# A decoder block in fp32r on one core: attention values issued one unit later, 83 unread matmuls fewer, and the early weight blocks split by ScalarE and VectorE

## The chip, the cores and the metric

The kernel runs on one core of a Trainium2 chip, alone. The time is the device time of one execution in microseconds. Before the change it is 3495.51 us, the median of three runs (3493.86 to 3495.92).

## What is computed

Two transformer-like blocks follow each other over 512 tokens of width 1024. The change touches only the first part of the first block, its mixer:

```python
u = rmsnorm(x, attn_norm_pre)
proj = u @ w_in                       # 27 blocks of 128 columns
fq, fk, fv, ff = split(p_fox)         # 8 heads of 64
o_fox = forgetting_attention(fq, fk, fv, ff, fox_forget_bias)
o_rwkv = rwkv7_time_mix(p_rwkv, ...)  # 8 heads of 64
mix = concat([o_fox, o_rwkv]) @ w_out # 8 blocks
h = x + rmsnorm(mix, attn_norm_post)
```

Forgetting attention is softmax attention with a bias from cumulated forget gates, causal. After the mixer come a gated feed-forward part and the whole second block (an HGRN2 and a retention mixer, and a PEER expert layer), whose code is the same before and after.

## The kernel before

**Storage.** Activations lie transposed, features on 128 partitions and 512 tokens along the free dimension, in an arena of 75 tiles. Weights stream from memory as blocks of 128x1024 values (512 KB) into a ring of four slots, `ring`. SyncE issues the load of block n when block n-4 has been used (semaphore `block_used`). Block numbers: 0 to 12 are the attention's input projection (`N_FOX` = 13), 13 to 26 the RWKV part's (`N_RW` = 14), 27 to 34 the output projection (`B_WOUT` = 27), and the feed-forward part starts at 35 (`B_FFN`).

**Splitting.** A product of two fp32 matrices is made from fp32r parts. Each block is rounded to `ring_hi`, and the remainder goes to `ring_lo`. `three` (lines 330 to 335) issues three matmuls per 128x128 piece and 512 tokens: hi by hi, hi by lo, lo by hi. A block is 8 pieces, so 24 matmuls. Who splits a block differs. Block 0 is rounded by ScalarE and its remainder taken by VectorE. Blocks 1 to 34 are split whole by GpSimd (`split`, lines 1410 to 1418, a multiplication by one and a subtraction for each). From block 35 on ScalarE rounds and VectorE subtracts (`dense` on either). `ready(n)` on TensorE (line 319) waits for the remainder.

**The order of the work.** Each engine has its program written out by hand, with semaphores between them.

1. TensorE multiplies block 0, then forms the sums of squares of the input norm (line 362, eight fp32 products with ones), whose squares ScalarE writes into two tiles by turns, then blocks 1 to 14. VectorE takes the norm's reciprocal root (line 1457) and multiplies each finished bank by it (`normed`, line 1495). For RWKV blocks it also shifts by one token and mixes (`shift`, lines 1498 to 1507, the largest operations on lines 1504 and 1506). Among these it works on the forget gates and copies masks (lines 1511 to 1537).
2. TensorE transposes the attention's values (line 403) and makes four rounds of low-rank products for RWKV (lines 409 to 418): two with 64 rows side by side (412, 415), one with 128 (417) and one with 32 (418). ScalarE applies tanh and sigmoid to their inputs and outputs.
3. Attention runs in 32 units u, head u // 4 and query block t = u % 4, with t + 1 key blocks. For each unit the engines do: TensorE the scores (`fox_scores`, lines 448 to 453), VectorE the maximum (1544), ScalarE exp with the row sum (`fox_exp`), VectorE reciprocal and scaling (1550, 1551), TensorE transposes of the probabilities (475), ScalarE the copy of these to SBUF (`fox_copy`), TensorE the product with the values (486). The loop on every engine is one unit ahead with the scores: `fox_scores(u + 1)`, `fox_out(u)`, `rw_prepare(u)`. `fox_out` holds both the transposes and the values, so TensorE waits for the copy in between. The last function prepares RWKV operands: in units 0 to 11 VectorE shifts a block there, in unit 13 TensorE makes 32 tiny head sums (494), and in units 14 to 30 there is a chain of elementwise work and now and then a transpose (502) or a product (519) on TensorE.
4. In units 0 to 11 TensorE also multiplies one RWKV input block, in four quarters around the transposes (`rw_quarter`). From unit 12 on there are none left, and `keep_clock` (lines 337 to 341) issues matmuls of 512 columns whose result is not read: 4 - t before the transposes and 4 - t after them, 100 in all.
5. After the units come the RWKV levels and chunks (lines 526 to 700, 357.6 to 489 us) with `keep_clock` calls of their own, the group norm, and the output projection (`w_out_block`). Its first half of inputs is the attention's, its second half RWKV's, which VectorE and ScalarE split chunk by chunk (`xs_lo`, line 1453) just before.

Helpers that record many operations: ScalarE's activations all have line 965.

Of the kernel before, what the change touches and what calls it, by code (L numbers as in the profile page):

```python
# [118 lines left out]
def build(nc, xt, par_d, cst_d, sel_d, rot_d, rmask_d, small_d, keys_d, wstream, gates_d, hidden_d, out):  # L119
    with ExitStack() as ctx:  # L120
# [91 lines left out]
        split_hi, dense_hi, dense_lo = sem("split_hi"), sem("dense_hi"), sem("dense_split")  # L212
# [103 lines left out]
        def _(pe):  # L316
            st = Steps(pe, pe_s)

            def ready(n, it=0, per=0):

                if n < B_FFN:
                    pe.wait_ge(w_split, it * per + (n + 1))
                elif n < B_U:
                    pe.wait_ge(dense_lo, it * per + (n - B_FFN + 1))
                elif n < B_S:
                    pe.wait_ge(w_split, it * per + (n - B_U + B_FFN + 1))
                else:
                    pe.wait_ge(u_lo, it * per + (n - B_S + 1))
# [127 lines left out]
            def fox_out(u):  # L456
                h, t = units[u]
                m, e = h // 2, h % 2
                bt, bo = bank[6 + u % 2], bank[2 + m % 2]
# [7 lines left out]
                if u >= N_RW - 2:  # L467
                    if u % 8 == 0:
                        pe.wait_ge(fo_out, m)
                    keep_clock(2 + (m + 1) % 2, 4 - t)  # L470
# [9 lines left out]
                if u >= N_RW - 2:  # L480
                    keep_clock(2 + (m + 1) % 2, 4 - t)
# [40 lines left out]
            for u in range(len(units)):  # L522
                if u + 1 < len(units):
                    fox_scores(u + 1)
                fox_out(u)
                rw_prepare(u)

# [433 lines left out]
        def _(act):  # L961
# [50 lines left out]
            for k in range(KD):  # L1012
                act.wait_ge(in_x[k // 2], 16)
                A(XS[k][0], xr(k), ACT.Copy, scale=pp("attn_pre", k)).then_inc(hi_ready, 1)
            for k in range(KD):
                norm_square(0, k, xr)
            norm_root(0)

# [3 lines left out]
            A(z, z, ACT.Ln, bias=1.0).then_inc(fc_ln, 1)  # L1022
            q = N_FOX + N_RW
# [27 lines left out]
            def fox_copy(u):  # L1051
# [6 lines left out]
                if h % 2 == 1 and t == TT - 1:  # L1058
                    act.wait_ge(fo_ready, u + 1)
                    m = h // 2  # L1060
                    A(tile(OF + m), bank[2 + m % 2][:, :], ACT.Copy).then_inc(fo_out, 1)

            def rw_prepare(u):

                if u == 12:
# [17 lines left out]
            for u in range(len(units)):  # L1083
                if u + 1 < len(units):
                    fox_exp(u + 1)
                fox_copy(u)
                rw_prepare(u)

# [41 lines left out]
            for k in range(4):  # L1130
                act.wait_ge(rw_dve, bd + 4 + k + 1)
                A(XS[4 + k][0], tile(ORW + k), ACT.Copy).then_inc(hi_ready, 1)
            for k in range(KD):
                if k == 4:
                    dense(B_FFN)
# [270 lines left out]
        def _(pool):  # L1406

            one = cst[:, CCOL["ones"][0]:CCOL["ones"][0] + 1].to_broadcast([P, D])

            def split(r, n, it, hi_done, lo_done, first=0):  # L1410

                pool.wait_ge(loaded[r], it * 16 + 16)
                pool.tensor_tensor(ring_hi[:, r, :], ring[:, r, :], one, ALU.mult).then_inc(hi_done, 1)
                pool.wait_ge(hi_done, n + 1)
                if first:
                    pool.wait_ge(lo_done, first)
# [3 lines left out]
            pool.wait_ge(in_cst, 16)  # L1420
            def remainder(r, n, lo_done):

                pool.wait_ge(dense_hi, n - B_FFN + 1)
                pool.tensor_tensor(ring_lo[:, r, :], ring[:, r, :], ring_hi[:, r, :].bitcast(F32), ALU.subtract  # L1424
                                   ).then_inc(lo_done, 1)

            pool.sem_inc(split_hi, 1)
            for r in range(1, RING):
                split(r, r, 0, split_hi, w_split, r)
            with pool.Fori(1, B_FFN // RING) as i:  # L1430
                for r in range(RING):
                    split(r, i * RING + r, i, split_hi, w_split)
# [708 lines left out]
```

## Time and profile before

| | |
|---|---|
| median of three runs | 3495.51 us |
| the profiled execution | 3498.85 us, span 3497.0 us |
| mean granted TensorE clock | 0.977 of 2.4 GHz |
| TensorE busy | 3373.8 us (96%) |
| VectorE, ScalarE, GpSimd busy | 1921.3, 1219.7, 286.6 us |
| chain that ended last | TensorE 85%, VectorE 11%, ScalarE 2% |

Times are microseconds from the first instruction unless marked ns. PE is TensorE, DVE VectorE, ACT ScalarE, POOL GpSimd, and L412 is line 412 of the kernel. The span and some 2 us around it make the execution's time. A matmul's printed duration includes its fill and drain, which overlap with the next one, so the distance of two starts tells what one costs. The granted clock is 1.00 when TensorE may run at 2.4 GHz and 0.50 at 1.2 GHz; a mean between says how the stretch is shared out. In brackets behind a row stands how long the engine had been idle before it, and what ended the idle time.

### The profile page before, as it was taken

The numbers are of one execution on the slowest core, as the hardware profiler recorded it, in microseconds if no ns is written. First come the engines' busy times: TensorE is split into PE (matmuls) and PEld (weight loads), VectorE is DVE, ScalarE is ACT, GpSimd is POOL, SyncE is SP. The second block draws the span as 40 slices with busy tenths as digits, with TensorE's granted clock in tenths as the row PEclk, the third lists the DMA queues.
The fourth block names the chain that finished last, engine by engine and source line by source line (L and its number), as shares of the span: only waits on it lengthen the run. The fifth ranks groups of instructions, "written<-read, shape, count | busy, mean of one in ns | idle before, by whom it ended". The sixth has DMA issues, their size and how long they took to land.

```text
span 3497.0 us, 50301 instructions
## 1 busy us (share of the span) xinstructions
PE 3373.8 (96%) x18594; PEld 2733.2 (78%) x18594; DVE 1921.3 (55%) x3675; ACT 1219.7 (35%) x1588; POOL 286.6 (8%) x122
## 2 busy tenths in 40 slices
PE   8999999999989999998999999999999899999998
PEld 6565786887667788887878888888888788888886
DVE  3565444553366633334245899998986344444443
ACT  2222223332355533333233443444444333333332
POOL 6440010000000000000000444100000000000000
PEclk9887999999999999999999999999999999999999
DMA  4110002332222222222323344455556765555542
GB/s 140 44 47 0 3 19 68 97 97 95 85 72 68 70 73 77 72 73 84 97 90 109 112 144 139 140 180 181 181 180 202 237 206 192 193 194 194 192 144 78
DMA packets 146028, 408.31 MB, mean 117 GB/s; under 512 B 11224, under 2 KB 43992, under 8 KB 143584
## 3 DMA queue, kind: packets, MB, share of 16 engines
q1 hardware_dynamic: 73520, 265.85, 25.1%
q10 hardware_dynamic: 72368, 140.68, 11.2%
q8 instruction: 77, 1.26, 0.1%
q14 instruction: 63, 0.52, 0.1%
HBM read 337.28 MB, written 69.21 MB: 116 GB/s over the span
## 4 chain that ended last, share of the span: by engine, by line
PE 85%; DVE 11%; ACT 2%; issue 1%; ACTq 1%; DMA 0%; DVEq 0%; SPq 0%
PE bank L333 23%; PE bank L335 23%; PE bank L334 23%; PE bank L924 2%; PE bank L429 2%; PE bank L922 2%; PE bank L362 1%; PE bank L858 1%; ACT arena L965 1%; DVE arena L1946 1%; PE bank L486 1%; PE bank L341 1%; PE bank L448 1%; DVE arena L1909 1%; DVE arena L1910 1%
## 5 line engine op out<-in xcount | busy, mean ns | idle before, releaser
L333 PE MATMUL bank<-xs,ring_hi 128*128 128x512 f32 x2488 | 998.0, 401 | 39.4 <-DVE xs L1453 13.8
L335 PE MATMUL bank<-xs,ring_lo 128*128 128x512 f32 x2488 | 975.4, 392 | 0.0
L334 PE MATMUL bank<-xs,ring_hi 128*128 128x512 f32 x2488 | 974.3, 392 | 0.0
L965 ACT ACTIVATE arena<-bank 128x512 f32<-128x512 f32 (+4 forms) x584 | 392.1, 705 | 1031.0 <-PE bank L335 736.6
L965 ACT ACTIVATE ring_hi<-ring 128x1024 fp32r<-128x1024 f32 x469 | 495.9, 1060 | 602.1 <-DMA ring<-weights 367.3
L333 PEld LDWEIGHTS bank<-xs,ring_hi 128*128 128x128 f32 x2488 | 471.2, 189 | 149.4 <-issue 24.8
L1707 DVE TENSOR_TENSOR ring_lo<-ring,ring_hi 128x1024 fp32r<-128x1024 f32 x212 | 258.5, 1224 | 538.6 <-ACT ring_hi L965 537.6
L334 PEld LDWEIGHTS bank<-xs,ring_hi 128*128 128x128 f32 x2488 | 471.6, 190 | 100.0 <-issue 5.3
L335 PEld LDWEIGHTS bank<-xs,ring_lo 128*128 128x128 f32 x2488 | 470.2, 189 | 101.5
L1959 DVE TENSOR_TENSOR ring_lo<-ring,ring_hi 128x1024 fp32r<-128x1024 f32 x206 | 252.4, 1225 | 386.1 <-ACT ring_hi L965 386.1
L333 PE MATMUL bank<-gw,ring_hi 128*128 128x512 f32 x1024 | 398.5, 389 | 0.7 <-ACT arena L965 0.7
L334 PE MATMUL bank<-gw,ring_hi 128*128 128x512 f32 x1024 | 398.3, 389 | 0.0
L335 PE MATMUL bank<-gw,ring_lo 128*128 128x512 f32 x1024 | 398.3, 389 | 0.0
L1424 POOL TENSOR_TENSOR ring_lo<-ring,ring_hi 128x1024 fp32r<-128x1024 f32 x50 | 131.7, 2633 | 1542.7 <-ACT ring_hi L965 1542.7
L333 PEld LDWEIGHTS bank<-gw,ring_hi 128*128 128x128 f32 x1024 | 192.3, 188 | 41.0 <-ACT arena L965 1.1
L335 PEld LDWEIGHTS bank<-gw,ring_lo 128*128 128x128 f32 x1024 | 192.3, 188 | 39.9
L334 PEld LDWEIGHTS bank<-gw,ring_hi 128*128 128x128 f32 x1024 | 192.3, 188 | 39.8
L1978 DVE TENSOR_SCALAR oneL<-cst,arena 128x128 fp32r<-128x128 f32 x512 | 175.4, 343 | 0.0
L1977 DVE TENSOR_SCALAR oneH<-cst,arena,ghi 128x128 fp32r<-128x128 f32 x512 | 175.3, 342 | 0.0
L965 ACT ACTIVATE gw<-arena 128x512 fp32r<-128x512 f32 x128 | 80.5, 632 | 228.9 <-DVE arena L1992 227.3
L1998 DVE TENSOR_TENSOR gw<-arena,gw 128x512 fp32r<-128x512 f32 x128 | 88.3, 692 | 90.8 <-ACT gw L965 90.8
L965 ACT ACT_TABLE_LOAD x89 | 114.2, 1283 | 18.3 <-PE bank L335 9.3
(281 smaller groups left out, 3689.2 us busy)
## 6 DMA issues: line engine op xcount, KB each, us to landing
ring<-weights SPq DMA_DIRECT2D x503, 512.0 KB, 3.6
hidden<-arena ACTq DMA_DIRECT2D x128, 256.0 KB, 4.1
gates<-arena ACTq DMA_DIRECT2D x16, 2048.0 KB, 6.6
arena<-hidden ACTq DMA_DIRECT2D x16, 2048.0 KB, 10.4
arena<-gates ACTq DMA_DIRECT2D x16, 2048.0 KB, 17.3
xres<-x_t ACTq DMA_DIRECT2D x4, 512.0 KB, 6.3
out_t<-arena SPq DMA_DIRECT2D x4, 512.0 KB, 2.9
arena<-ret_decay ACTq DMA_DIRECT2D x1, 1024.0 KB, 5.9
```

What stands on the lines that cost most here:

```text
L333: pe.matmul(out_, wh, x[0], start=start, stop=False, skip_group_check=True)
L334: pe.matmul(out_, wh, x[1], start=False, stop=False, skip_group_check=True)
L335: return pe.matmul(out_, wl, x[0], start=False, stop=stop, skip_group_check=True)
L429: mm = pe.matmul(quad(dst, p, j, g), quad(l, p, j, g), quad(r, p, j, g), start=True, stop=True, skip_group_check=True)
L922: pe.matmul(dst, oneH[:, u % NHOT, j, :], oneB[:, u % NHOT, j, :], start=True, stop=False, skip_group_check=True)
L965: return act.activation(out_, in_, f, **kw)
L1424: pool.tensor_tensor(ring_lo[:, r, :], ring[:, r, :], ring_hi[:, r, :].bitcast(F32), ALU.subtract).then_inc(lo_done, 1)
L1707: TTN(ring_lo[:, r, :], ring[:, r, :], ring_hi[:, r, :].bitcast(F32), ALU.subtract).then_inc(dense_lo, 1)
L1959: TTN(ring_lo[:, r, :], ring[:, r, :], ring_hi[:, r, :].bitcast(F32), ALU.subtract).then_inc(u_lo, 1)
L1977: TSM(oneH[:, u % NHOT, j, :], iota, key1, ghi[:, 0, t1].bitcast(F32), ALU.is_equal, ALU.mult)
L1978: ins = TSM(oneL[:, u % NHOT, j, :], iota, key1, arena[:, PTT + 2, t1], ALU.is_equal, ALU.mult)
L1998: TTN(GW[b][j][1], tile(HV + 8 * b + j), GW[b][j][0].bitcast(F32), ALU.subtract).then_inc(ex_lo, 1)
```

## The change

On TensorE, the product with the values leaves `fox_out` and becomes `fox_values`, issued for unit u - 1 behind the scores of unit u + 1 and ahead of the transposes of unit u. Of the unread matmuls one per unit stays, ahead of the transposes, in units 13 to 31 except 16 and 24: 17 instead of 100. ScalarE's copy of a finished pair of heads moves behind the exp of the next unit. GpSimd's splitting of blocks 1 to 34 is deleted. ScalarE rounds them and VectorE takes the remainders, at places written into their programs, and `dense_hi` and `dense_lo` now count from block 1.

```diff
@@ TensorE, ready and fox_out
-                if n < B_FFN:
-                    pe.wait_ge(w_split, it * per + (n + 1))
+                if n == 0:
+                    pe.wait_ge(w_split, 1)
                 elif n < B_U:
-                    pe.wait_ge(dense_lo, it * per + (n - B_FFN + 1))
+                    pe.wait_ge(dense_lo, it * per + n)
...
-                if u >= N_RW - 2:
-                    if u % 8 == 0:
-                        pe.wait_ge(fo_out, m)
-                    keep_clock(2 + (m + 1) % 2, 4 - t)
+                if u > N_RW - 2 and u % 8:
+                    keep_clock(2 + (m + 1) % 2, 1)
                 pe.wait_ge(fnorm, u + 1)
...
-                if u >= N_RW - 2:
-                    keep_clock(2 + (m + 1) % 2, 4 - t)
+
+            def fox_values(u):
+                h, t = units[u]
+                m, e = h // 2, h % 2
+                bo = bank[2 + m % 2]
                 pe.wait_ge(ft_out, u + 1)
...
             for u in range(len(units)):
                 if u + 1 < len(units):
                     fox_scores(u + 1)
+                if u:
+                    fox_values(u - 1)
                 fox_out(u)
                 rw_prepare(u)
+            fox_values(len(units) - 1)
@@ ScalarE
+            dense(1)
+            dense(2)
             for k in range(KD):
                 norm_square(0, k, xr)
             norm_root(0)
+            for n in range(3, N_FOX):
+                dense(n)
...
             A(z, z, ACT.Ln, bias=1.0).then_inc(fc_ln, 1)
+            for n in range(N_FOX, N_FOX + 4):
+                dense(n)
...
             def rw_prepare(u):
 
+                if u < N_RW:
+                    dense(N_FOX + 4 + u)
...
+                if u and u % 8 == 0:
+                    pair_copy(u // 8 - 1)
                 fox_copy(u)
                 rw_prepare(u)
+            pair_copy(NPAIR - 1)
...
+            dense(B_WOUT + 4)
+            dense(B_WOUT + 5)
             for k in range(KD):
+                if k == 2:
+                    dense(B_WOUT + 6)
                 if k == 4:
+                    dense(B_WOUT + 7)
                     dense(B_FFN)
@@ GpSimd
-            pool.sem_inc(split_hi, 1)
-            for r in range(1, RING):
-                split(r, r, 0, split_hi, w_split, r)
-            with pool.Fori(1, B_FFN // RING) as i:
-                for r in range(RING):
-                    split(r, i * RING + r, i, split_hi, w_split)
-            for n in range(B_FFN // RING * RING, B_FFN):
-                split(n % RING, n, n // RING, split_hi, w_split)
@@ VectorE
+            def dense(n, it=0, per=0):
+
+                r = n % RING
+                ve.wait_ge(dense_hi, it * per + n)
+                TTN(ring_lo[:, r, :], ring[:, r, :], ring_hi[:, r, :].bitcast(F32), ALU.subtract).then_inc(dense_lo, 1)
+
...
+            dense(1)
             ve.wait_ge(in_cst, 16)
             norm_root(0)
+            dense(2)
...
             for n in range(8):
                 normed(n, tile(Q0 + n), bank[n % NBANK])
+                dense(n + 3)
             shift(8, 0)
+            dense(11)
...
             for n in range(11, N_FOX):
                 normed(n, tile(VF0 + n - 9), bank[n % NBANK])
+                dense(n + 3)
...
             shift(N_FOX, 1)
+            dense(N_FOX + 3)
             shift(N_FOX + 1, 2)
...
                 if 1 <= u <= N_RW - 2:
                     shift(N_FOX + 1 + u, 2 + u)
+                if u < N_RW:
+                    dense(N_FOX + 4 + u)
...
+            for n in range(B_WOUT + 4, B_FFN):
+                dense(n)
             for b in range(3):
                 dense(B_FFN + b)
```

## Rows read from the trace of the kernel before

**Rows 1.** Windows: PE, PEld, DVE, ACT, POOL busy; granted clock; DMA share; GB/s

```profile
100.50:133.80 33.30, 27.24 (x60) 9.15 (x58) 9.68 (x9) 12.74 (x22) 8.07 (x4) 0.63 0.05 16
133.80:229.00 95.20, 95.20 (x427) 69.91 (x426) 66.96 (x92) 13.29 (x38) 51.46 (x22) 0.98 0.20 61
...
246.00:357.60 111.60, 99.76 (x337) 57.83 (x338) 54.21 (x126) 28.05 (x72) 0.00 (x0) 0.74 0.00 1
357.60:489.00 131.40, 125.02 (x3723) 109.92 (x3722) 56.15 (x99) 31.39 (x59) 0.00 (x0) 1.00 0.01 4
```

**Rows 2.** Groups, TensorE, 246 to 357.6 us: busy, mean ns | idle before

```profile
L341 PE MATMUL bank<-ring_hi 128*128 128x512 f32 x86 | 34.9, 508 | 0.0
...
L475 PE MATMUL bank<-cst,arena 128*128 128x128 f32 x47 | 11.4, 355 | 9.9 <-DVE arena L1551 9.5
```

**Rows 3.** Timeline, low-rank products: start, duration, engine, line [idle before]

```profile
100.55 1.91 PE L403 MATMUL bank<-cst,arena 128*128 128x128 f32 x16
105.97 1.17 PE L412 MATMUL bank<-arena 64*128 64x512 f32 x1 [3.51 <-ACT arena L965]
...
110.59 2.07 PE L417 MATMUL bank<-arena 128*128 128x512 f32 x2 [2.55 <-ACT arena L965]
...
120.61 1.22 PE L412 MATMUL bank<-arena 64*128 64x512 f32 x1
...
126.62 1.22 PE L412 MATMUL bank<-arena 64*128 64x512 f32 x1
...
130.29 1.12 PE L418 MATMUL bank<-arena 32*128 32x512 f32 x2
```

**Rows 4.** Timeline, VectorE: one operation without and beside GpSimd's work

```profile
71.50 0.75 DVE L1506 SCALAR_TENSOR_TENSOR arena<-arena,par 128x512 f32<-128x512 f32 x1
...
101.98 2.65 DVE L1506 SCALAR_TENSOR_TENSOR arena<-arena,par 128x512 f32<-128x512 f32 x1
```

**Rows 5.** Timeline, the start

```profile
15.01 1.89 POOL L1413 TENSOR_TENSOR ring_hi<-ring,cst 128x1024 fp32r<-128x1024 f32 x1 [14.56 <-DMA ring<-weights]
...
17.09 7.42 PE L362 MATMUL bank<-arena,cst 128*128 128x512 f32 x16
...
19.29 1.90 POOL L1413 TENSOR_TENSOR ring_hi<-ring,cst 128x1024 fp32r<-128x1024 f32 x1
...
23.94 0.79 PE L333 MATMUL bank<-xs,ring_hi 128*128 128x512 f32 x1
...
25.43 3.35 DVE L1457 RECIPROCAL arena<-arena 128x512 f32<-128x512 f32 x1 [11.42 <-ACT arena L965]
```

**Rows 6.** Page's groups: a block rounded by ScalarE, remainder by VectorE

```profile
L965 ACT ACTIVATE ring_hi<-ring 128x1024 fp32r<-128x1024 f32 x469 | 495.9, 1060 | 602.1 <-DMA ring<-weights 367.3
...
L1707 DVE TENSOR_TENSOR ring_lo<-ring,ring_hi 128x1024 fp32r<-128x1024 f32 x212 | 258.5, 1224 | 538.6 <-ACT ring_hi L965 537.6
```

**Rows 7.** Timeline, units 12 and 13

```profile
239.27 0.69 PE L475 MATMUL bank<-cst,arena 128*128 128x128 f32 x2 [2.71 <-DVE arena L1551]
...
242.21 3.88 PE L494 MATMUL bank<-cst,arena 128*128 128x2 f32 x32
```

**Rows 8.** Timeline, unit 17, TensorE at 2.4 GHz

```profile
268.08 0.91 PE L341 MATMUL bank<-ring_hi 128*128 128x512 f32 x3
269.54 0.44 PE L475 MATMUL bank<-cst,arena 128*128 128x128 f32 x2 [0.55 <-DVE arena L1551]
269.73 0.94 PE L341 MATMUL bank<-ring_hi 128*128 128x512 f32 x3
...
271.19 1.12 PE L519 MATMUL bank<-arena,cst 128*128 128x512 f32 x2
```

**Rows 9.** Timeline, unit 29, TensorE at 1.2 GHz

```profile
344.44 0.69 PE L475 MATMUL bank<-cst,arena 128*128 128x128 f32 x2
...
347.38 1.58 PE L519 MATMUL bank<-arena,cst 128*128 128x512 f32 x2
```

**Rows 10.** Timeline, end of the mixer: TensorE waiting for VectorE

```profile
515.94 0.79 PE L333 MATMUL bank<-xs,ring_hi 128*128 128x512 f32 x1 [0.95 <-DVE xs L1453]
```

More of the change, by code:

```diff
@@ L211, in build @@
         w_split = sem("weights_split")
-        split_hi, dense_hi, dense_lo = sem("split_hi"), sem("dense_hi"), sem("dense_split")
+        dense_hi, dense_lo = sem("dense_hi"), sem("dense_split")
         first_hi = sem("first_block_hi")
@@ L319, in ready @@
             def ready(n, it=0, per=0):
-                if n < B_FFN:
-                    pe.wait_ge(w_split, it * per + (n + 1))
+                if n == 0:
+                    pe.wait_ge(w_split, 1)
                 elif n < B_U:
-                    pe.wait_ge(dense_lo, it * per + (n - B_FFN + 1))
+                    pe.wait_ge(dense_lo, it * per + n)
                 elif n < B_S:
-                    pe.wait_ge(w_split, it * per + (n - B_U + B_FFN + 1))
+                    pe.wait_ge(w_split, it * per + (n - B_U + 2))
                 else:
@@ L458, in fox_out @@
                 m, e = h // 2, h % 2
-                bt, bo = bank[6 + u % 2], bank[2 + m % 2]
+                bt = bank[6 + u % 2]
                 if u == 0:
@@ L1057, in fox_copy, with pair_copy @@
                 A(tile(PT0 + u % 2)[:, 0:n], bank[6 + u % 2][:, 0:n], ACT.Copy).then_inc(ft_out, 1)
[L1058 to L1061, printed above, removed]
+            def pair_copy(m):
+                act.wait_ge(fo_ready, 8 * (m + 1))
+                A(tile(OF + m), bank[2 + m % 2][:, :], ACT.Copy).then_inc(fo_out, 1)
             def rw_prepare(u):
+                if u < N_RW:
+                    dense(N_FOX + 4 + u)
                 if u == 12:
@@ L1406, in _, with remainder @@
         def _(pool):
[L1408 to L1416, printed above, removed]
+            def remainder(r, n, lo_done):
+                pool.wait_ge(dense_hi, n)
                 pool.tensor_tensor(ring_lo[:, r, :], ring[:, r, :], ring_hi[:, r, :].bitcast(F32), ALU.subtract
                                    ).then_inc(lo_done, 1)
[L1420 to L1425, printed above, removed]
-            pool.sem_inc(split_hi, 1)
-            for r in range(1, RING):
-                split(r, r, 0, split_hi, w_split, r)
-            with pool.Fori(1, B_FFN // RING) as i:
-                for r in range(RING):
-                    split(r, i * RING + r, i, split_hi, w_split)
-            for n in range(B_FFN // RING * RING, B_FFN):
-                split(n % RING, n, n // RING, split_hi, w_split)
             first = -(-B_U // RING)
@@ L1526, in _ @@
                 normed(n, tile(VF0 + n - 9), bank[n % NBANK])
+                dense(n + 3)
             ve.wait_ge(in_small, 32)
@@ L1702, in _ @@
             xs_lo(1, lambda k: tile(ORW + k - 4), KD - 1)
-            def dense(n, it=0, per=0):
-                r = n % RING
-                ve.wait_ge(dense_hi, it * per + (n - B_FFN + 1))
-                TTN(ring_lo[:, r, :], ring[:, r, :], ring_hi[:, r, :].bitcast(F32), ALU.subtract).then_inc(dense_lo, 1)
+            for n in range(B_WOUT + 4, B_FFN):
+                dense(n)
             for b in range(3):
```

## The prediction

> **What bounds the kernel now.** The windows view comes first, for the granted clock and the busy time by stage. All the code that changes runs before 533 us; what follows is only shifted. TensorE is busy for nearly all of every stretch [rows 1], so a gain must come from idle time of TensorE, from work taken off it, or from a better clock. Two stretches stand out. From 100.5 to 133.8 us (low-rank products) the clock averages 0.63 of 2.4 GHz, and from 246 to 357.6 us (attention units 14 to 31) it averages 0.74. In the second, the groups by line show what fills TensorE: 86 unread matmuls (line 341) and a wait of 9.9 us for VectorE's probabilities [rows 2]. In the low-rank stretch the timeline shows TensorE waiting 3.51 us for an activation and 2.55 us for the next one [rows 3]. Those follow VectorE's token shift, whose last operation takes 2.65 us beside GpSimd's splitting and 0.75 us alone [rows 4]. GpSimd is off the path by its own busy time, yet it stretches operations that are on it.
>
> **The change, part by part.** Times are those of the profiled execution: span 3497.0, whole 3498.9, which is 3.3 above the median of the runs, 3495.5.
>
> *A. The start.* Block 1 landed at 15.0 (GpSimd's wait ends there); block 2 had landed by 19.29, when GpSimd took it up without idle time [rows 5]. ScalarE now splits both before it squares the inputs, and it does so in order, so the first square waits for block 2's landing. A copy takes 1.06 us and a remainder 1.22 [rows 6]. The squares start between 16.1 (block 2 already there) and 20.4. I take a landing midway, 17.2, so squares from 18.2 and the first of the eight summing products at 18.9 instead of 17.1. Their pace, 7.4 us for the eight, is set by the exchange of two buffers and stays. Block 1 starts 1.8 later. Behind the root, VectorE runs the reciprocal (3.35 us, beginning 1.5 after block 1 starts [rows 5]) and only then block 2's remainder. That ends 6.1 us after block 1 began, while a block takes 5.45 (14 of them lie between 23.94 [rows 5] and 100.55 [rows 3]), so block 2 waits 0.7 or 0.8. Cost: **+2.6** (bounds 0 and +5). From there to 100.5 TensorE never waits. A block takes 5.45 us, while VectorE needs 0.7 for the evacuation and 1.2, and ScalarE 1.1, for each, so the steady part is worth nothing either way. If that cover were gone, each late microsecond would count once for each of 25 blocks.
>
> *B. The low-rank stretch.* Without GpSimd, VectorE's shift step falls from 5.0 us to about 2.4 (the operation of [rows 4] is the largest part of that), and the casts and small copies ahead of them get shorter too. The remainders added, 1.2 us for each block, take back less than that. The shift of block 13 then ends some 3 us before block 14 does. The 3.51 us wait goes, and of the 2.55 us some 0.5 stay (ScalarE has four copies and a sigmoid to do). More follows. Before, the clock was at 2.4 GHz up to this idle time and at 1.2 GHz after it, and the stretch ran so until 130. A round took 6.0 us (120.61 to 126.62, like two of the other three [rows 3]), and the only product that ran at 2.4 GHz, line 418 in the last round, took 1.05 us (130.29 to 131.34) instead of 2.0. If the idle time is gone I expect the clock to hold, as it held until this idle time: rounds of 3.05. New: 2.0 for the transposes, 1.0, 0.5, 2.05, three more rounds 9.15, and 2.3 for the first two units' scores, together 17.0 against 33.3. Gain: **16.2**. At the other bound the clock falls anyway: 3 × 3.0 + 2.5 less, so 4.7.
>
> *C. Units 0 to 11.* TensorE carries a block per unit and is busy 95.2 of 95.2 us in just under 12 units, 8.0 for each [rows 1]. ScalarE gets a copy and VectorE a remainder, while VectorE's shift loses some 3 us, so it has less to do than before. The one new wait is VectorE's for ScalarE's copy, which is behind the unit's transposes in the middle of the unit. Queued behind it is the next maximum, and behind that the probabilities for which TensorE's transposes wait. By my count the remainder ends 7.4 us into a unit of 8.0, and the next maximum is not wanted for another 2. Hidden: **0** (a gain is excluded because TensorE has no wait to lose). SP issues the same loads at the same block counts.
>
> *D. Units 12 and 13.* Transposes of unit 13 wait 2.71 us for VectorE, whose shift has an operation of 2.7 us beside GpSimd there as in the stage before [rows 4, 7]. The shift shrinks by 2 to 4 us and a remainder adds 1.2. The fillers and values between unit 12's transposes and the next scores (2.4 us) and, in unit 13, the 2.9 us between transposes (239.27) and head sums (242.21) leave the front [rows 7]. I get transposes 3.0 earlier and head sums 5.6 earlier: **5.6** (bounds 3 and 7). The head sums still precede a stretch at 1.2 GHz.
>
> *E. Units 14 to 31.* The values of unit u-1 now run while VectorE makes the probabilities of unit u, and of 86 fillers 16 remain. In unit 17 the scores end where line 341 starts, 268.08; transposes follow at 269.54, a filler again 0.19 later, and the next stage at 271.19 [rows 8]. The gap before the transposes, 1.46 us, is VectorE's (maximum, reciprocal, scaling) and stays. It takes in 0.36 of values and one filler of 0.23. Behind the transposes 1.65 shrink to 0.2: 1.45 gained. At 1.2 GHz, unit 29 has 2.94 there [rows 9] and keeps 0.35: 2.6 gained. The other 16 units have the same pattern with one to four blocks. Two prices go against it. VectorE's preparation (2.2 to 2.7 us) now reaches past the next scores in every second unit at 2.4 GHz, 0.75 each. At 1.2 GHz the values of a four-block unit (1.9) overfill the gap. Averaged over the four kinds, a unit of 5.2 us at 2.4 GHz becomes 4.0, and one of 7.7 at 1.2 GHz becomes 5.4. The old mean, 111.6 / 18 = 6.2, is 60% of the first and 40% of the second, which makes half of the time slow, as the clock of 0.74 says. With the fillers gone the clock will be low more often. I take two thirds of the units: 4.93 × 18 = 88.7, and 4 for unit 31's late values and the roots of unit 14: 92.7. Gain: **19** (bounds 10 with all at 1.2 GHz, 33 with nearly all at 2.4). It is a judgement that the share goes from 40% to 67%, since the old 0.74 had 34.9 us of fillers in it.
>
> Here a rule of the Trainium skill speaks against the change. "TensorE: Matmul & The Clock Gate", section "A second HAM failure mode: psum-queue depth-cycling", says that TensorE's short idle times between groups of matmuls make its clock swing, and that the throughput pays for it. By that rule all 18 units would be slow, and the gain 10 instead of 19, which is the second rival. The trace agrees that the clock swings here, at 0.74 even with the fillers.
>
> *F. The output projection.* VectorE's split of the mixer's output is stretched beside GpSimd like its shifts, and TensorE waits for it twice, a microsecond each, after the second time at 1.2 GHz [rows 10]. Without GpSimd the chunks are ready before they are wanted: two waits and three chunks at half clock, **3.9** (bounds 2 and 4). Blocks 31 to 34 are copied by ScalarE ahead of its evacuations. Each has landed some 4 us after its slot came free and is wanted 5 to 15 us later: 0.
>
> Sum: +2.6 - 16.2 - 5.6 - 19.0 - 3.9 = -42.1, so 3498.9 - 42.1 = 3456.8, or 3454 at the scale of the median.
>
> **The rivals.**
> 1. *The clock falls in the low-rank stretch all the same.* For it: the stretch stayed at 1.2 GHz for 20 us although TensorE was busy, so these products do not bring the clock back and may not hold it. Against it: the fall came after idle time. B gives 4.7: 3466.
> 2. *Units 14 to 31 sit at 1.2 GHz* for want of fillers: E gives 10.4 instead of 19: 3463. For it: 0.74 with fillers [rows 1]. Against it: the same work is packed into less time, which the fillers had been padding.
> 3. *They stay at 2.4 GHz*, the denser schedule making up for the fillers: E gives 33 or so, 3440.
> 4. *VectorE binds in units 0 to 11*, because the remainder waits for ScalarE's copy behind the transposes. One microsecond in each of 12 units: 3466.
> 5. *Slower.* Without fillers the clock does not come back after unit 31, and the RWKV levels and chunks, 357.6 to 489, run at 1.2 GHz. They are 125 us of TensorE work in 131.4 at clock 1.00 [rows 1], so all of it would cost up to 125: 3579. From 42 us, a third of the stretch, the gain is eaten. Against it: that stretch is dense and has fillers of its own.
>
> That the split does not move is excluded by the diff, and GpSimd's part there is deleted.
>
> **How the numbers follow.** Forecast (A to F as summed) 0.52; rival 1 0.15; rival 2 0.15; rival 3 0.08; rival 4 0.06; rival 5 0.04. A measurement of this kernel can tell about 0.2%, 7 us, from no change. All cases but the fifth are faster by more, and of the fourth a part could be worse than priced: faster 0.94, same 0.02, slower 0.04. The range goes from rival 3 with a little more in A, 3438, to rivals 1 and 2 together, 3474.
>
> **What would show it.** Right: no GpSimd work before the expert blocks; line 1506 of before at 0.75 us throughout; 100.5 to 133.8 at a clock near 1.0 and about 17 us long, after a start 2 to 3 us later; a unit of 4 to 5.5 us after 14 with transposes waiting for the scaling; units 0 to 11 still 8.0. Wrong: a low clock after the 16 transposes, TensorE waiting for remainders in units 0 to 11, or a clock under 1.0 past unit 31.

## The result, and the profile after

| | before | after |
|---|---|---|
| median of 5 runs each | 3495.51 us (3479.96 to 3498.06) | 3456.26 us (3453.43 to 3460.98) |
| ratio | | 0.9897, 95% interval 0.9881 to 0.9913 |
| profiled execution, span | 3498.85, 3497.0 | 3453.43, 3451.6 |
| clock, mean | 0.977 | 0.981 |

The changed kernel is 1.0% faster. The forecast was 3454 us. The profiled execution after is the fastest of its five, and that of before lay 3.3 us above the median, so the two profiles are 45.4 us apart and the medians 39.3.

The page's busy times after. GpSimd is down from 122 operations to 54, all of them far behind this stage; TensorE has 83 instructions fewer, the unread matmuls (100 before, 17 now).

```profile
PE 3342.3 (97%) x18511; PEld 2717.8 (79%) x18511; DVE 1904.2 (55%) x3709; ACT 1253.7 (36%) x1622; POOL 131.7 (4%) x54
```

The windows of the changed kernel (columns as in [rows 1]): the low-rank stretch up to the first quarter of a block, units 14 to 31, the RWKV levels and chunks, the output projection.

```profile
102.76:119.89 17.13, 16.83 (x59) 6.76 (x58) 2.64 (x6) 11.44 (x19) 0.00 (x0) 1.00 0.10 31
229.07:316.18 87.11, 81.37 (x272) 46.46 (x271) 53.66 (x126) 27.65 (x72) 0.00 (x0) 0.70 0.00 1
318.50:449.00 130.50, 124.40 (x3715) 109.14 (x3714) 55.86 (x98) 30.86 (x59) 0.00 (x0) 1.00 0.02 4
449.00:494.00 45.00, 45.00 (x206) 35.78 (x205) 20.72 (x30) 16.66 (x24) 0.00 (x0) 0.96 0.18 59
```

Against [rows 1]: the low-rank stretch has halved and its clock went from 0.63 to 1.00. Units 14 to 31 shrank from 111.6 to 87.1 us, with a clock that did not rise (0.74, then 0.70). The RWKV levels and chunks behind them did not change (131.4 and 130.5 us in these windows, both at 1.00); the output projection did, by some 5 us (step F below).

The timeline at the start. The first copy waits for block 1's landing and the second for block 2's, so the summing products (L362) start at 18.82 (17.09 before) and block 1 (L333) at 25.75 (23.94).

```profile
14.83 1.06 ACT L969 ACTIVATE ring_hi<-ring 128x1024 fp32r<-128x1024 f32 x1 [2.45 <-DMA ring<-weights]
17.10 1.06 ACT L969 ACTIVATE ring_hi<-ring 128x1024 fp32r<-128x1024 f32 x1 [1.21 <-DMA ring<-weights]
18.82 7.49 PE L362 MATMUL bank<-arena,cst 128*128 128x512 f32 x16 [0.94 <-ACT arena L969]
25.75 0.80 PE L333 MATMUL bank<-xs,ring_hi 128*128 128x512 f32 x1
```

The low-rank products on TensorE. Of the waits of 3.51 and 2.55 us [rows 3] only 0.30 is left, and rounds follow each other in 3.17 us where they took 6.0.

```profile
102.76 1.91 PE L403 MATMUL bank<-cst,arena 128*128 128x128 f32 x16
104.60 0.69 PE L412 MATMUL bank<-arena 64*128 64x512 f32 x1
...
106.03 1.13 PE L417 MATMUL bank<-arena 128*128 128x512 f32 x2 [0.30 <-ACT arena L969]
...
108.14 0.69 PE L412 MATMUL bank<-arena 64*128 64x512 f32 x1
...
111.30 0.69 PE L412 MATMUL bank<-arena 64*128 64x512 f32 x1
...
117.63 0.49 PE L448 MATMUL bank<-arena 64*128 64x128 f32 x2
```

Units 12 and 13. The wait for VectorE is 1.77 us (2.71 in [rows 7]), but the 32 head sums (L495) now take 6.34 us instead of 3.88: the clock falls half a microsecond into them, and the window from their start to the next scores has a mean of 0.54.

```profile
220.26 0.49 PE L341 MATMUL bank<-ring_hi 128*128 128x512 f32 x1
222.52 0.44 PE L473 MATMUL bank<-cst,arena 128*128 128x128 f32 x2 [1.77 <-DVE arena L1562]
222.79 6.34 PE L495 MATMUL bank<-cst,arena 128*128 128x2 f32 x32
229.07 2.07 PE L448 MATMUL bank<-arena 64*128 64x512 f32 x2
```

```profile
222.79:229.07 6.28, 6.28 (x34) 6.26 (x33) 3.74 (x4) 2.61 (x3) 0.00 (x0) 0.54 0.00 0
```

### The profile page after: what moved, and what is told of

Its sections match the earlier page's. It is cut to its first block, busy times and chain, and to the rows that moved or that the text cites. A ratio compares the mean times of both kernels' runs of the same rounds, so it can differ in the third digit from the quotient of the medians.

```text
span 3451.6 us, 50061 instructions
## 1 busy us (share of the span) xinstructions
PE 3342.3 (97%) x18511; PEld 2717.8 (79%) x18511; DVE 1904.2 (55%) x3709; ACT 1253.7 (36%) x1622; POOL 131.7 (4%) x54
## 4 chain that ended last, share of the span: by engine, by line
PE 85%; DVE 11%; ACT 2%; issue 1%; ACTq 1%; DMA 1%; DVEq 0%; SPq 0%
PE bank L333 24%; PE bank L335 23%; PE bank L334 23%; PE bank L928 2%; PE bank L429 2%; PE bank L926 2%; PE bank L362 1%; PE bank L862 1%; ACT arena L969 1%; DVE arena L1956 1%; DVE arena L1919 1%; DVE arena L1920 1%; DVE arena L1922 1%; PE bank L448 1%; DVE arena L1954 1%
## 5 line engine op out<-in xcount | busy, mean ns | idle before, releaser
L333 PE MATMUL bank<-xs,ring_hi 128*128 128x512 f32 x2488 | 997.4, 401 | 37.8 <-DVE xs L1452 11.8
L969 ACT ACTIVATE ring_hi<-ring 128x1024 fp32r<-128x1024 f32 x503 | 531.7, 1059 | 660.6 <-DMA ring<-weights 423.2
L1486 DVE TENSOR_TENSOR ring_lo<-ring,ring_hi 128x1024 fp32r<-128x1024 f32 x246 | 300.0, 1224 | 563.3 <-ACT ring_hi L969 562.2
L333 PEld LDWEIGHTS bank<-xs,ring_hi 128*128 128x128 f32 x2488 | 470.3, 189 | 149.2 <-issue 26.8
L1969 DVE TENSOR_TENSOR ring_lo<-ring,ring_hi 128x1024 fp32r<-128x1024 f32 x206 | 252.3, 1225 | 386.9 <-ACT ring_hi L969 386.7
L333 PE MATMUL bank<-gw,ring_hi 128*128 128x512 f32 x1024 | 398.5, 389 | 0.7 <-ACT arena L969 0.7
L333 PEld LDWEIGHTS bank<-gw,ring_hi 128*128 128x128 f32 x1024 | 192.2, 188 | 40.9 <-ACT arena L969 1.1
```

The source lines that it names most:

```text
L333: pe.matmul(out_, wh, x[0], start=start, stop=False, skip_group_check=True)
L969: return act.activation(out_, in_, f, **kw)
L1486: TTN(ring_lo[:, r, :], ring[:, r, :], ring_hi[:, r, :].bitcast(F32), ALU.subtract).then_inc(dense_lo, 1)
L1969: TTN(ring_lo[:, r, :], ring[:, r, :], ring_hi[:, r, :].bitcast(F32), ALU.subtract).then_inc(u_lo, 1)
```

## The experiments

Twelve kernels were run, each against the kernel before on the same chip. "Split" says who splits blocks 1 to 34: GpSimd, or ScalarE and VectorE as in the changed kernel (new). "Values" says whether a unit's product with the values stands right behind its own transposes (at once) or one unit later (late). "D" is the time from unit 13's scores to unit 15's, "E" from there to the transposes behind unit 31, both from the profiled execution, with E's granted clock. "Unread" counts the unread matmuls in units 12 to 31. D and E are of one execution each. That execution lay within 5 us of its kernel's median, save for start_order (7.8 above) and attn_only (7.2 below).

| kernel | split | values | unread | D | E, clock | median us | ratio, 95% interval |
|---|---|---|---|---|---|---|---|
| before | GpSimd | at once | 100 | 16.0 | 111.6, 0.74 | 3495.5 | 1 |
| split_only | new | at once | 100 | 12.4 | 105.8, 0.81 | 3467.2 | 0.9916 (0.9900 to 0.9933) |
| filler_only | new | at once | 17 | 17.2 | 125.6, 0.54 | 3494.1 | 0.9991 (0.9981 to 1.0001) |
| attn_only | GpSimd | late | 17 | 15.9 | 86.2, 0.72 | 3473.5 | 0.9939 (0.9922 to 0.9955) |
| changed kernel | new | late | 17 | 13.6 | 87.1, 0.70 | 3456.3 | 0.9897 (0.9881 to 0.9913) |
| no_unread | new | late | 0 | 13.0 | 89.6, 0.63 | 3459.2 | 0.9900 (0.9884 to 0.9915) |
| once_ahead | new | late | 42 | 12.8 | 78.8, 0.85 | 3443.5 | 0.9849 (0.9835 to 0.9862) |
| order_only | new | late | 92 | 12.0 | 80.8, 0.96 | 3444.8 | 0.9854 (0.9837 to 0.9870) |
| start_order | new, new start | late | 92 | 12.0 | 82.1, 0.94 | 3440.8 | 0.9843 (0.9830 to 0.9857) |
| unfed_once | new, new start | late | 49 | 12.0 | 78.8, 0.85 | 3436.1 | 0.9842 (0.9823 to 0.9860) |
| fed_once | new, new start | late | 57 | 16.0 | 75.5, 0.89 | 3438.6 | 0.9837 (0.9823 to 0.9851) |
| fed_full | new, new start | late | 100 | 14.9 | 81.4, 0.95 | 3443.7 | 0.9852 (0.9836 to 0.9868) |
| fed_one | new, new start | late | 38 | 14.6 | 87.2, 0.70 | 3457.5 | 0.9880 (0.9859 to 0.9902) |
| pool_beside | new, GpSimd busy | late | 17 | 14.3 | 90.5, 0.65 | 3468.6 | 0.9926 (0.9907 to 0.9944) |

### The two parts, each alone

**split_only** is the changed kernel with attention's order and unread matmuls as before. The diff is against the changed kernel (the values' matmuls stand in fox_out again, the pair's copy in fox_copy):

```
-                if u > N_RW - 2 and u % 8:
-                    keep_clock(2 + (m + 1) % 2, 1)
+                if u >= N_RW - 2:
+                    if u % 8 == 0:
+                        pe.wait_ge(fo_out, m)
+                    keep_clock(2 + (m + 1) % 2, 4 - t)
...
+                if u >= N_RW - 2:
+                    keep_clock(2 + (m + 1) % 2, 4 - t)
...
-                if u:
-                    fox_values(u - 1)
```

> The early weight blocks split by ScalarE and VectorE as in the changed kernel; attention's order, its unread matmuls and the pair copies as before. Theory: the steps of the changed trace add up, so this one carries the start (+2.2 us), the low-rank stretch (-16), units 0 to 11 (-0.6) and the output projection (-5): about -19.5 us, 3476 us (3472 to 3480), and its low-rank rounds take 3.2 us each at granted clock 1.00. Rival: the low-rank stretch is faster only because everything near it moved with the attention part; then its rounds are still 6 us and the kernel gains only some 4 us, 3491 us.

3467.2 us: 29.6 below before in its series, 10 more than the steps allow. The low-rank rounds are 3.2 us at 1.00, as expected. Most of the surplus stands in units 12 to 31 although their code is before's: D 12.4 for 16.0, and E 105.8 for 111.6 with a clock of 0.81 for 0.74. Another 8.4 us lie behind unit 31 (there, 3467.4 - 336.4 against 3497.0 - 357.6), where the steps had 5: 5.6 in the output projection, as in the changed kernel, 0.9 in the RWKV stage, and 1.9 in all that follows. What follows is the same code in every kernel here and took between 2938.6 and 2942.6 us in their profiles, so the 1.9 says nothing.

**attn_only** is before's code with the attention part of the diff and nothing else.

> Only the attention part: values one unit later, one unread matmul in each late unit; GpSimd still splits the early blocks. Theory of added steps: units 14 to 31 give their -24.5 us and units 12 and 13 some -3: 3468 us (3464 to 3472); the low-rank rounds stay at 6.0 us each. Rival: the two parts help each other (the clock at the entry into unit 14 depends on the split), then the gain here is under 20 us, over 3476 us.

3473.5 us, between the two: the gain is 23.3. E is 86.2, as in the changed kernel. The first low-rank round and most of the second run at the low clock, the last two at 2.4 GHz (L412 at 105.45, 113.89, 119.19, 122.35), so the stretch from the first transpose to the first scores was 25.5 us long and before's 30.8, though its code and its wait of 3.52 us were the same. Most of the 5.3 us between them are the clock's. The parts alone give 29.6 and 23.3, together 39.3: they overlap.

### The attention part taken apart

**order_only** and **filler_only** fill the square: with the new split, the order of the values and the number of unread matmuls are changed one at a time. In order_only (the second hunk stands behind the unit's own transposes):

```
-                if u > N_RW - 2 and u % 8:
-                    keep_clock(2 + (m + 1) % 2, 1)
+                if u >= N_RW - 2 and u % 8:
+                    keep_clock(2 + (m + 1) % 2, 4 - t)
...
+                if u >= N_RW - 2:
+                    if u % 8 == 0:
+                        pe.wait_ge(fo_out, m)
+                    keep_clock(2 + (m + 1) % 2, 4 - t)
```

> As the changed kernel, but with the unread matmuls of before (4 less the row of the unit, twice in each unit from unit 12 on; a wait for the pair's copy stands ahead of them at a pair's first unit). Only the order of the values differs from before there. Theory 1: the removed unread matmuls, some 70 of 0.23 to 0.43 us that stood on TensorE's path, are most of the gain of the late units: this kernel loses 12 to 20 us against the changed one, 3468 to 3476 us. Rival: the values' wait for ScalarE's copy of the transposes was what bounded a unit; then the unread matmuls only fill idle time and this kernel is within 5 us of the changed one, up to 3461 us.

3444.8 us: faster than the changed kernel, with intervals to before that do not touch. Both expectations were wrong, and Theory 1 in its sign.

filler_only has before's order (values behind the unit's own transposes) and the changed kernel's single unread matmul:

> As the changed kernel, but each unit's values stand right behind its own transposes, as before, with the one unread matmul ahead of the transposes: only the removal of unread matmuls differs from before in the late units. Theory 1: TensorE then waits 0.7 to 0.9 us in each of 20 units for ScalarE's copy of the transposes, some 15 us more than the changed kernel, 3466 to 3474 us. Rival: those waits also lower the granted clock in the late units below 0.6 for the stretch, and it costs 25 us or more, 3481 us or more, close to no gain from the removal at all.

3494.1 us, no longer distinguishable from before: the rival holds, with a clock of 0.54. The windows of units 14 to 31 in the three kernels, in the order split_only, order_only, filler_only:

```profile
230.54:336.35 105.81, 92.82 (x338) 54.21 (x337) 54.55 (x127) 28.05 (x72) 0.00 (x0) 0.81 0.00 1
```

```profile
229.07:309.84 80.77, 77.55 (x334) 45.60 (x333) 55.33 (x128) 27.66 (x72) 0.00 (x0) 0.96 0.00 1
```

```profile
233.62:359.17 125.55, 101.36 (x268) 53.57 (x267) 54.21 (x126) 28.08 (x72) 0.00 (x0) 0.54 0.00 0
```

The second kernel gives TensorE 66 instructions more than the third, and keeps it busy for 24 us less. In medians, which come from different series (the kernel before lies between 3492.9 and 3496.8 in them): the late values are worth 22.4 us with 100 and 92 unread matmuls (3467.2 to 3444.8) and 37.8 with 17. Taking unread matmuls out costs 26.9 in the old order (3467.2 to 3494.1) and 11.5 in the new (3444.8 to 3456.3). **So half of the attention part wins and the other half gives back part of it.**

**once_ahead** puts `4 - t` for `1` into the changed kernel's line and lets it begin with unit 12 instead of 13, **no_unread** deletes the line.

> As the changed kernel, with 4 less the row of the unit unread matmuls ahead of the transposes where it has one, and none behind them: about half of before's number. Theory 1, formed on the last runs: in the late units the unread matmuls pay for themselves by the granted clock (0.96 of units 14 to 31 with before's number, 0.70 with one each), so half the number gives a clock between and 3446 to 3454 us. Rival: half the number already holds the clock at 0.9 or more, at half the price; then this is the fastest kernel so far, 3430 to 3440 us.

> As the changed kernel, without any unread matmul in the late units. Theory 1: TensorE's clock falls further, to about 0.55 in units 14 to 31, and the kernel loses 5 to 15 us against the changed one, 3461 to 3471 us. Rival, the view of the prediction: an unread matmul on TensorE's path only costs its own time; then leaving out 16 of 0.23 to 0.43 us gains 4 to 6 us, 3450 to 3452 us.

42 unread matmuls: 3443.5, a little under Theory 1's range, as good as 92. None: 3459.2, whose interval overlaps with the changed kernel's, so the last 17 neither cost nor gain what can be measured. Theory 1's direction of the clock holds (0.63), its price was too high, and the rival's gain is not there. The windows of units 14 to 31, first once_ahead, then no_unread:

```profile
230.03:308.83 78.80, 74.40 (x290) 42.97 (x289) 53.86 (x127) 27.72 (x72) 0.00 (x0) 0.85 0.00 1
```

```profile
231.88:321.46 89.58, 80.34 (x256) 46.49 (x255) 53.95 (x126) 27.72 (x72) 0.00 (x0) 0.63 0.00 1
```

The trade can be read off the same four units, at clock 1.00 but for half a microsecond in the changed kernel. They take 15.4 us with one unread matmul each (changed kernel, scores at 260.29 and 275.68) and 15.5 with ten in the four (once_ahead, 261.68 and 277.22): those ten stand where TensorE would wait for VectorE, and cost nothing. With twenty they take 17.5 (order_only, 256.92 and 274.43). But four units with a mixed clock take 19.8 (changed kernel, 275.68 to 295.46), and once_ahead has none of these behind 254 us.

### GpSimd beside VectorE

**pool_beside** leaves the new split as it is and adds work for GpSimd whose result nobody reads:

```
+            pool.memset(arena[:, 63:65, :], 1.0).then_inc(beside, 1)
+            pool.wait_ge(beside, 1)
+            for n in range(2, 24):
+                pool.wait_ge(block_used, n)
+                for c in range(2):
+                    pool.tensor_tensor(arena[:, 63:65, :], arena[:, 63:65, :], arena[:, 63:65, :], ALU.mult).then_inc(beside, 1)
+                    pool.wait_ge(beside, 2 * (n - 2) + c + 2)
```

VectorE waits in unit 13 until these 45 operations are done; nothing waits for them before that.

> The changed kernel, and GpSimd multiplies 128x1024 of ones in a place that nothing reads, twice behind every block from the second to the 23rd, as often as it split blocks before. Nothing waits for the results before unit 13. Theory 1: VectorE's shifts and remainders beside it take three times as long (2.3 to 2.7 us for 0.75), TensorE waits ahead of the low-rank products, its clock falls there, and the stretch from the eight passes to the first quarter takes 24 to 33 us in place of 17: 3463 to 3474 us. Rival: it was the late results of GpSimd that counted, not its work beside VectorE; then this is the changed kernel's 3456 us within 2.

3468.6 us, as Theory 1 has it. The stretch takes 24.3 us (104.45 to 128.78). VectorE's timeline in it, then one line of GpSimd's and one of TensorE's:

```profile
99.40 1.86 DVE L1551 COPY cst<-cst 64x64 f32<-64x64 f32 x1
101.30 1.93 DVE L1552 COPY cst<-cst 64x64 f32<-64x64 f32 x1
103.26 0.19 DVE L1553 COPY cst<-cst 64x64 f32<-64x64 f32 x1
...
105.20 0.69 DVE L1510 TENSOR_TENSOR arena<-bank,arena 128x512 f32<-128x512 f32 x1
105.92 1.55 DVE L1519 TENSOR_TENSOR arena<-arena 128x511 f32<-128x511 f32 x1
107.39 0.14 DVE L1520 TENSOR_SCALAR arena<-arena 128x1 f32<-128x1 f32 x1
107.57 2.20 DVE L1521 SCALAR_TENSOR_TENSOR arena<-arena,par 128x512 f32<-128x512 f32 x1
...
99.32 3.87 POOL L1433 TENSOR_TENSOR arena<-arena 128x1024 f32<-128x1024 f32 x2 [2.14 <-PE bank L335]
...
111.73 1.19 PE L412 MATMUL bank<-arena 64*128 64x512 f32 x1 [5.37 <-DVE arena L1510]
```

A 64x64 copy takes 0.19 us alone and 1.86 or 1.93 beside GpSimd, which is one of GpSimd's two operations (3.87 / 2). TensorE then waits 5.37 us, and the first round runs at the low clock (111.73 to 117.03, against 3.17 for the next). The Trainium skill, "SBUF — State Buffer", section "SBUF: two separate sides", says that the two engines lock a shared pair of ports for a whole instruction and that the other one blocks. These rows agree: the copy's duration is that of the GpSimd operation, not its own made some factor longer.

### Start and head sums

**start_order** is order_only with

```
+            norm_square(0, 0, xr)
+            norm_square(0, 1, xr)
             dense(1)
             dense(2)
-            for k in range(KD):
+            for k in range(2, KD):
```

on ScalarE, and `dense(2)` ahead of `norm_root(0)` on VectorE.

> Before's unread matmuls in the new order of values (the kernel of the run at 3445 us), and at the start ScalarE takes the first two squares ahead of its copies of blocks 1 and 2, VectorE the remainder of block 2 ahead of its reciprocal. Theory: the ones-matmuls start 0.9 us earlier and the 0.45 us wait for block 2 goes, together 1 to 2.5 us: 3442 to 3444 us. Rival: the squares are bound by their hand-over with TensorE from the third on, which starts as late as ever: no change, 3445 us.

3440.8 us. The intervals overlap with order_only's; in the profile the summing products start at 17.93 (18.75) and the low-rank products at 103.23 (104.57), so 1.3 us are shown and the rest of the 4 is not.

**fed_once**, **fed_full** and **fed_one** have this start, all of before's unread matmuls in units 12 and 13, two more behind each pair's eight head sums, and 4 - t once, 4 - t twice or 1 in each unit from 14 on. **unfed_once** is fed_once without those at the head sums.

```
                         head_sums(1, m, tile(DT4[m])).then_inc(rw_pe, 1)
+                        keep_clock(2, 2)
```

> The start of the last run (first squares ahead of blocks 1 and 2); units 12 and 13 with before's unread matmuls, two more unread matmuls behind each pair's head sums (8), and from unit 14 on half of before's number (4 less the row, ahead of the transposes, none at a pair's first unit). Theory 1: the 32 head sums of two columns let the clock fall at 229 to 230 us in every kernel with unread matmuls, and it takes 7 us (before's number) to 20 us (half of it) to come back; fed there, it stays at 1.00 through units 14 to 31, which then take some 72 us in place of 79: 3431 to 3437 us. Rival: the head sums have nothing to do with it, the clock falls there anyway, and the 8 extra ones only cost 1 to 2 us: 3442 to 3446 us.

> As the kernel fed at the head sums, but with before's full number of unread matmuls from unit 14 on. Theory 1: both hold the clock at 1.00, so this one pays for its 40 further unread matmuls, as far as they do not fill waits: 3434 to 3442 us, 3 to 6 us slower than with half. Rival: half the number loses the clock again now and then; this one is then the faster.

> As the kernel fed at the head sums, but from unit 14 on with the changed kernel's single unread matmul. Theory 1: the clock starts unit 14 at 1.00 but falls again within a few units, since each unit's waits for VectorE are left open: mean clock 0.70 to 0.85 in units 14 to 31, 3446 to 3452 us. Rival: what lowered the clock in the changed kernel was only the entry by the head sums; once it is up, one unread matmul holds it, units 14 to 31 take under 72 us and this is the fastest, 3427 to 3433 us.

The feed did not hold the clock, so Theory 1 fails in all three: fed_once is 3438.6, fed_full 3443.7, fed_one 3457.5. D was 14.6 to 16.0 us with the feed and 12.0 without it. In fed_one the fall to 0.70 with one unread matmul came as expected, at a time above the range. Its clock came back at 244 us, as fed_once's did, and then fell three more times, where fed_once's stayed up until 302: what holds the clock in units 14 to 31 is the unread matmuls there, not the entry. order_only, then fed_full, around and behind the head sums:

```profile
225.52:229.07 3.55, 3.55 (x33) 3.54 (x31) 2.65 (x3) 2.12 (x2) 0.00 (x0) 1.00 0.00 0
229.07:236.00 6.93, 6.93 (x18) 3.57 (x17) 4.11 (x9) 3.08 (x6) 0.00 (x0) 0.53 0.00 0
```

```profile
222.53:227.86 5.33, 5.33 (x40) 5.06 (x38) 3.75 (x4) 2.11 (x2) 0.00 (x0) 0.91 0.00 0
227.86:236.23 8.37, 8.37 (x19) 4.18 (x19) 3.00 (x7) 3.00 (x6) 0.00 (x0) 0.50 0.01 2
```

> The new start, units 12 and 13 with before's unread matmuls, half of before's number from unit 14 on, and nothing behind the head sums: the kernel fed at the head sums without the 8 extra unread matmuls, whose clock fell all the same. Theory: the 8 saved are 1 to 3 us: 3435 to 3438 us, the fastest. Rival: they brought the clock back earlier inside units 14 to 18 even though it fell, as its return at 245 us against 253 us without them suggests; then this one is at 3440 to 3443 us, no better than the kernels without the feed.

3436.1 us, the lowest median of all and within the theory's range, though its interval overlaps those of fed_once, start_order and once_ahead. It is 0.5% under the changed kernel by the medians of the two series (3436.1 / 3492.9 against 3456.3 / 3495.5 gives 0.9837 against 0.9888), and their intervals to before do not touch. Its units 14 to 31 read like once_ahead's:

```profile
225.00:233.00 8.00, 8.00 (x23) 4.42 (x23) 4.54 (x10) 3.49 (x7) 0.00 (x0) 0.55 0.00 0
233.00:241.00 8.00, 8.00 (x29) 6.05 (x29) 2.24 (x9) 2.54 (x8) 0.00 (x0) 0.50 0.01 2
241.00:249.00 8.00, 8.00 (x18) 3.74 (x16) 5.13 (x11) 1.82 (x5) 0.00 (x0) 0.50 0.00 1
249.00:257.00 8.00, 7.37 (x35) 4.44 (x34) 5.29 (x13) 1.96 (x6) 0.00 (x0) 0.96 0.00 0
```

## Why the prediction was right, and where it was not

By the boundaries of the two profiled executions (first low-rank transpose, first scores, scores of units 13 and 15, transposes behind unit 31, last root of the output projection's stage). F takes in the RWKV stage, which was 0.4 longer:

| step | predicted | measured |
|---|---|---|
| A start | +2.6 | 102.76 - 100.55 = +2.2 |
| B low-rank stretch | -16.2 | 14.87 - 30.79 = -15.9 |
| C units 0 to 11 | 0 | 97.87 - 98.65 = -0.8 |
| D units 12, 13 | -5.6 | 13.57 - 16.03 = -2.5 |
| E units 14 to 31 | -19.0 | 87.11 - 111.58 = -24.5 |
| F output projection | -3.9 | -46.6 + 41.4 = -5.2 |
| behind it | 0 | -45.4 + 46.6 = +1.2 |

**A** held by its own steps: block 2's landing set the first square (its copy starts at 17.10, forecast 17.2), and block 2 waited 0.5 us for the remainder behind the reciprocal (forecast 0.7 or 0.8).

**B** held, with its mechanism shown by pool_beside: GpSimd's work alone, without any of its results being wanted, brings back the slow shifts, the wait and a round at the low clock. Rival 1 is false: the clock stays at 1.00 when the idle time goes. attn_only adds that the low clock does end inside these dense products, which the prediction had doubted. It also shows that the size rests in part on luck: the new stretch came out as forecast (14.87 us, 14.7 without the scores), but the old one took 30.8 us in before's profile and 25.5 in attn_only's.

**C** held: TensorE is busy for 89.86 of 89.86 us between 125.64 and 215.50, so rival 4 is false. Rival 5 is false by the window up to 449 us.

**D** was mis-sized and fell below its bounds of 3 and 7. Counted from unit 13's scores, its transposes came 2.3 earlier (forecast 3.0) and the head sums 4.9 (forecast 5.6). The head sums were to last as long as before; the step took no account of the clock under them. Of the 14 unread matmuls of units 12 and 13 one was left, the clock fell half a microsecond into the head sums, behind the wait of 1.77 us, and they took 6.34 us for 3.88. In order_only, with those 14 kept, they take 3.63 and D is 12.0, a gain of 4.0. The unread matmuls that D counted as gain were what part of the gain depended on.

**E** came within its bounds and between the forecast and rival 3. The step took 12 units at 5.4 us and 6 at 4.0, which is 73% of the time at half clock and a mean of 0.64; the measured 0.70 is 60%. With the step's own unit times that share gives 89.3 us, an estimate, so some 3 of the 5.5 us beyond the forecast are the clock and the rest the units (3.85 us each at 1.00). The failure is in its attribution. It counted 1.45 us per unit as gained behind the transposes, mostly unread matmuls, and added them up as work off the path. The runs show the late values alone giving 105.8 - 80.8 = 25.0 in E, and the removal then taking back 6.3 (80.8 to 87.1): at full clock it saves 2.1 us in four units, and the clock costs more than that (0.96, then 0.70). Rival 2 named this cost but priced it against 19 instead of asking whether the removal was worth doing at all.

The rule that the prediction cited for it, from "TensorE: Matmul & The Clock Gate", section "A second HAM failure mode: psum-queue depth-cycling" of the Trainium skill, speaks of a clock that swings between its two levels where TensorE has short idle times. The changed kernel's units do that (up at 240 us, down at 247, up at 261, down at 281, up at 295, down at 302); that all 18 would be slow was the prediction's reading of it. In four kernels that differ in the unread matmuls alone, the clock goes with TensorE's idle time in E: 3.2 us at 0.96 (order_only), 4.4 at 0.85 (once_ahead), 5.7 at 0.70 (changed kernel), 9.2 at 0.63 (no_unread). Across the kernels it does not: split_only has 13.0 us idle at 0.81, and pool_beside 5.0 at 0.65. So the idle time is not shown to be what the clock follows; that the unread matmuls raise it is.

**F** held in its mechanism and passed its bound of 4; TensorE is busy for 45.00 of 45.00 us there, and the two waits of [rows 10] are gone. Of its surplus the clock explains the most: behind the group norm's 32 head sums TensorE ran at 1.2 GHz for 6.75 us before and for 3.5 us after, which is 1.6 us of work. That is not the change's doing. In attn_only, with before's split, it was 3.5 us as well, and in start_order and fed_one, with the new split, 6.75. The +1.2 behind it is inside the spread of that part (2938.6 to 2942.6 us in the fourteen profiles).

That the total came so near has luck in it. E gave 5.5 us more than forecast, D 3.1 less, and some 5 us of B and 1.6 of F are, by attn_only's trace, what before's profiled execution happened to lose to the clock. The profiles differ by 45.4 and the medians by 39.3, with the 42.1 of the sum between them. The two parts also overlap, which the sum did not allow for: on before's attention the split is worth 29.6, on the new order 17.2 (3473.5 to 3456.3), close to A + B + C + F = -19.7. In the profiles the extra on before's attention lies in E (5.8, where the new order gives the split nothing: 86.2, then 87.1), a little in D (3.7 against 2.3), and behind unit 31 (8.4 against 2.0). Of the last 6.4 about 3 are time at 1.2 GHz in the output projection, and 3 fall in code that is the same. Why the split raises the clock of E in the old order was not tested.

## What to carry to other kernels

Before an unread matmul is taken out, see whether it stands where TensorE would wait: here ten such matmuls in four units cost nothing, and the kernel that had them kept its clock once it was up. Reordering and the removal of unread matmuls should be timed apart; here one gained 22 us and the other lost 11, and the sum looked like success. When an engine off the path works beside VectorE, look for operations on small tiles whose duration is that of the other engine's instruction.

## What was not expected of the hardware

- The clock fell with TensorE busy. In order_only it was busy for 3.55 of 3.55 us at 1.00 over the 32 head sums and then for 6.93 of 6.93 us at 0.53, so idle time does not explain this fall. The clock fell in or behind these sums in eleven of the fourteen kernels; in filler_only, attn_only and pool_beside it was low before them. Two matmuls of 512 columns behind each eight did not prevent it (0.50 over 8.37 us in fed_full).
- The group norm's 32 sums of the same shape have 512-column matmuls on both sides, and the same happened there, in twelve of the fourteen kernels (not in no_unread and unfed_once). The rows are the kernel before: ahead of the sums, the sums, behind them. This speaks for the two-column products rather than the shapes behind them, but no run replaced them, so it is not shown.

```profile
489.00:495.36 6.36, 6.36 (x26) 3.89 (x22) 4.61 (x8) 4.79 (x7) 0.00 (x0) 1.00 0.00 1
495.36:499.16 3.80, 3.80 (x34) 3.80 (x32) 0.55 (x1) 0.11 (x1) 0.00 (x0) 0.92 0.02 4
499.16:505.00 5.84, 5.84 (x16) 4.57 (x17) 1.79 (x5) 0.29 (x1) 0.00 (x0) 0.50 0.00 0
```

- The clock can stay low for long with TensorE busy: in unfed_once 24 of 24 us from 225 to 249, nearly all at 1.2 GHz. When it came back does not follow the number of unread matmuls (237 us in order_only, 241 in start_order with as many, 250 in unfed_once, 254 in once_ahead, and 240 in the changed kernel with 17). Whether it stayed does: once back it held to unit 31 in order_only, start_order, once_ahead, unfed_once and fed_full, and with one unread matmul in a unit or none it fell again three times or more.
- The eviction from PSUM at 105.20 took its usual 0.69 us beside GpSimd, while the next operation, with both inputs in SBUF, took 1.55 for 0.69.
- One kernel's time can spread more where the clock swings: fed_one's five runs lie between 3445 and 3463 us, unfed_once's between 3433 and 3440.
